# Two steps of a recurrent stage's key normalisation move by one level each, on TensorE and on VectorE

## What is computed

```python
def wkv_scan(state0, r, dec, k, v, kk, a, reverse):
    def step(S, inp):
        d_t, k_t, v_t, kk_t, a_t = inp[:5]
        sa = jnp.einsum("bhvk,bhk->bhv", S, -kk_t)
        S = (S * d_t[:, :, None, :] + sa[..., None] * (kk_t * a_t)[:, :, None, :]
             + v_t[..., None] * k_t[:, :, None, :])
        out = jnp.einsum("bhvk,bhk->bhv", S, inp[5])
        return S, out
```

```python
    kk = heads(k * k_k).astype(jnp.float32)
    kk = kk * lax.rsqrt(jnp.sum(kk * kk, axis=-1, keepdims=True) + 1e-12)
```

## Time and profile before

| | us |
|---|---|
| median of 3 runs (4238.46 to 4240.1) | 4239.78 |
| the profiled execution | 4227.17 |
| its span, first to last instruction | 4225.4 |
| the recurrent stage's 120 levels in it, at 2353 to 3057 | 704 |

### The profile page before, as it was taken

One profiled execution on the slowest core, in us unless ns is written; L12 is line 12 of the kernel. 1 busy time (PEld: TensorE's weight loads), 2 busy tenths in 40 slices (PEclk: granted clock), 3 DMA queues, 4 the chain that ended last, 5 costly groups with the idle time before them and its releaser, 6 DMA issues. The chain is left out here.

```text
span 4225.4 us, 73949 instructions
## 1 busy us (share of the span) xinstructions
PE 3967.2 (94%) x32724; PEld 2597.9 (61%) x32724; DVE 1985.2 (47%) x3187; ACT 953.8 (23%) x1726; POOL 739.3 (17%) x598
## 2 busy tenths in 40 slices
PE   7999999999999999999998788888899999999997
PEld 2458886454788855555555677777754555554443
DVE  2547813365585149734101355555423544541593
ACT  2411100010120020021003443434213434430102
POOL 0024542000444410001001222332010100002000
PEclk9999999999999999999998999999999999999999
DMA  1123323432442212012223311111101111111121
GB/s 62 41 95 139 111 89 139 150 120 99 141 149 80 70 53 67 30 40 92 101 77 130 108 45 38 34 34 34 77 34 52 47 51 54 48 58 49 60 70 40
DMA packets 119124, 317.98 MB, mean 75 GB/s; under 512 B 12128, under 2 KB 79712, under 8 KB 107296
## 3 DMA queue, kind: packets, MB, share of 16 engines
q1 hardware_dynamic: 113040, 291.37, 19.8%
q0 software_dynamic: 5776, 22.03, 1.6%
HBM read 276.67 MB, written 30.41 MB: 73 GB/s over the span
## 5 line engine op out<-in xcount | busy, mean ns | idle before, releaser
L782 PE MATMUL lin_ps<-hn,ring 128*128 128x512 f32 (+1 forms) x4384 | 1457.1, 489 | 24.3 <-ACT arena L1650 8.8
L782 PEld LDWEIGHTS lin_ps<-hn,ring 128*128 128x128 f32 x4384 | 829.2, 190 | 604.0 <-issue 542.9
L782 PE MATMUL lin_ps<-arena,ring 128*128 128x256 f32 (+2 forms) x3056 | 950.4, 468 | 9.6 <-DVE arena L2589 7.6
L782 PEld LDWEIGHTS lin_ps<-arena,ring 128*128 128x128 f32 (+1 forms) x3056 | 577.8, 190 | 358.8 <-issue 305.4
L782 PE MATMUL lin_ps<-arena 64*64 64x64 f32 (+3 forms) x9432 | 623.0, 254 | 68.6 <-ACT arena L1650 30.6
L1650 ACT ACTIVATE arena<-lin_ps 128x512 f32<-128x512 f32 (+4 forms) x533 | 280.4, 546 | 1272.2 <-PE lin_ps L782 1271.9
L782 PEld LDWEIGHTS lin_ps<-arena 64*64 64x64 f32 (+1 forms) x9432 | 466.6, 142 | 158.9 <-issue 88.3
L2198 DVE SCALAR_TENSOR_TENSOR arena<-arena,vec 128x512 f32<-128x512 f32 (+3 forms) x499 | 386.5, 858 | 149.3 <-PE lin_ps L782 148.0
L782 PE MATMUL sum_ps<-arena 64*64 64x64 f32 (+1 forms) x7176 | 313.1, 223 | 34.9 <-issue 23.0
L2198 DVE SCALAR_TENSOR_TENSOR arena<-arena,cs 128x512 f32<-128x512 f32 x336 | 327.1, 1044 | 0.0
L782 PEld LDWEIGHTS sum_ps<-arena 64*64 64x64 f32 (+1 forms) x7176 | 263.2, 136 | 45.8 <-issue 27.7
(11 more groups left out here) (219 smaller groups left out, 3711.4 us busy)
## 6 DMA issues: line engine op xcount, KB each, us to landing
ring<-w_up SPq DMA_DIRECT2D x32, 1024.0 KB, 5.8
ring<-w_down SPq DMA_DIRECT2D x32, 1024.0 KB, 5.0
arena<-w_mod SPq DMA_DIRECT2D x24, 1024.0 KB, 7.8
arena<-w_mod SPq DMA_DIRECT2D x12, 2048.0 KB, 7.6
ring<-w_attn SPq DMA_DIRECT2D x16, 1536.0 KB, 6.7
ring<-w_conv_in SPq DMA_DIRECT2D x16, 1024.0 KB, 5.8
ring<-features SPq DMA_DIRECT2D x40, 384.0 KB, 3.4
features<-arena POOLq DMA_DIRECT2D x32, 384.0 KB, 2.6
```

Source lines behind the costliest of these rows:

```text
L782: return pe.matmul(out, lhsT, rhs, start=start, stop=stop)
```

## The change

Two tuples in the two `aside` functions:

```diff
@@ TensorE, aside(G, l)
                 if j + 1 < KD:
                     if (gg, l) == (0, 1):
                         key_sums(j + 1)
-                    if (gg, l) in ((0, 3), (0, 5)):
+                    if (gg, l) in ((0, 4), (0, 5)):
                         key_spread(j + 1, l // 5)
@@ VectorE, aside(G, l)
                     if (gg, l) == (0, 4):
                         keys(j + 1, 0)
-                    if (gg, l) == (1, 2):
+                    if (gg, l) == (1, 1):
                         keys(j + 1, 1)
```

## The result

| | before | change |
|---|---|---|
| median of five executions each, us | 4239.43 | 4197.07 |
| lowest to highest | 4233.45 to 4240.10 | 4192.83 to 4203.18 |
| the profiled execution | 4227.17 | 4203.18 |
| 120 levels of the stage, first to last level_z, in the profiled execution | 703.9 | 678.6 |
| TensorE's "issue" waits in the stage | 51.8 | 63.9 |

The ratio is 0.9908, with a 95% interval of 0.9897 to 0.9918. The change is faster by 42.4 us between medians, by some 39 us by the ratio. I had forecast 30.0 us and a range that ended at 4201: right in direction, too small in size. Two later comparisons gave 0.9917 (0.9904 to 0.9931) and 0.9904 (0.9886 to 0.9922), 32.5 and 39.4 us between medians. Two executions of the kernel before in those comparisons, of 5312.98 and 14702.32 us, ran in a slow state and are in none of the medians and means given here.

A forecast was written before the change was run, and what follows sets the result against it. TensorE, busy 94% of the span, was taken as the bound, its idle waits as lost time. Terms 12.2 + 13.5 + 7.6 + 3.7 = 37.0 us freed, less 7.0: 4239.8 - 30.0 = 4209.8 us, range 4201 to 4221.

The forecast's parts named there:

- The two waits: TensorE's waits on the reciprocal at (0,3) and the keys at (1,2) would go, freeing 12.2 and 13.5 us.
- The row that was to show the order: New TensorE waits on the keys would disprove 0.9 us of room; waits on L2696 or L2701 would show VectorE late.
- The spread's own time: The spread's 1.09 us would fall into 1.29 us of idle time ahead of level 5, freeing 7.6 us.
- GpSimd: Its wait on the keys would go from 24.6 us to near 0, worth 0 because TensorE never waits on it.
- The hold: New TensorE waits for instruction blocks behind the moved spread, one of mean length per cycle, would give back 7.0 us.
- The clock: Falls to 1.2 GHz behind the wait at (0,3), in three of seven cycles, would go, freeing 3.7 us.
- From profile to median: The profiled execution lay 12.6 us under the median; the same 30.0 us was taken off the median, giving 4209.8 us.

The follow-up runs named there:

- the shifted blocks: The change with 128 more TensorE instructions, half a block, in idle time ahead of its untouched recurrent stage; measured 0.9916 (0.9894 to 0.9939) of the kernel before.
- The repeated kernel before: The kernel before, run again with no edit; measured median 4233.73 us, ratio 0.9997 (0.9988 to 1.0006).
- the two repeats: The kernel before and the change, each run again with no edit; measured medians 4233.73 us and 4201.67 us.
- The spread alone: The kernel before with only the spread of part 0 moved from (0,3) to (0,4), keys left at (1,2); measured 0.9957 (0.9945 to 0.9969).
- the keys alone: The kernel before with only the second half of the keys moved from (1,2) to (1,1), spread left at (0,3); measured 0.9955 (0.9943 to 0.9967).

## Why the prediction was right or wrong

- **The two waits** (12.2 and 13.5 us): right, both gone, in every profile with the move. The row that was to show the order, no new wait on the keys or on late merges: right.
- **The spread's own time** (7.6 us): right. By the table of waits it looks smaller: the masks' waits went (2.2 us), ScalarE's shrank by 0.50 us in seven cycles (3.5 us), together 5.7 us. But the time from the start of one product to the start of another says more. From the last product of E at (0,4) to that at (0,5) it is 6.7 to 6.9 us before. In the change, with the spread between them, it is 6.7 us in five of the seven cycles; in the other two new holds of 0.67 and 1.01 us stand in it. So the spread costs nothing at its new place, and at (0,3) the stretch without its waits is shorter by 1.1 to 1.2 us (in cycles 1 and 2, at 2.4 GHz throughout, 2.8 instead of 3.95 us). Where products overlap, waits shrink by less than the time of the work that fills them.
- **GpSimd** no longer waits for the keys, and none of TensorE's waits named it before or after, as said. For what it may mean to VectorE see the last section.
- **The hold** (7.0 us): the mechanism was right and is now shown by the shifted blocks and the packets. Behind the spread, from the end of (0,3) to the end of (0,4), the "issue" waits grew by 6.2 us, near the 7.0. But the sum had no holds behind the moved keys, and from (1,2) to (1,4) they grew by 5.3 us; in all it is 12.1 us in the profile. The prediction took two neighbouring ends of blocks to be 3.7 us apart at the least; with waits at both, they come as close as 3.4 us. It is also here that the rule of the Trainium skill cited in the prediction (Runtime: NRT & Kernel Launch, section Instruction fetch mechanics) fails for this kernel: crossing a block is hidden at 96 of 165 ends in the change's stage, and the other 69 cost 63.9 us.
- **The clock** (3.7 us, bounds 0 and 3.7): this step failed. I counted falls in one execution, behind (0,3) only, and called their number the upper bound. The repeated kernel before has 44.4 us at 1.2 GHz in its stage, not 20.5, and five of its falls stand behind the keys' wait at (1,2), which the sum gave no clock at all. The changed kernel has 13.7 to 17.1 us. At 0.35 us for each, the clock gave 1.2 us between the first two profiles and 10.7 us between the two repeats.
- **From profile to median**: here the failed step turned into the miss. "since nothing here depends on the run, I take the same off the median": the profiled execution lay 12.6 us under the median of its kernel, and that difference was in large part made of what the change removes. The hint stood in the table, and I read it as a constant.

Net: without the clock the sum would be 12.2 + 13.5 + 7.6 - 7.0 = 26.3 us. The stages of the profiles give 21 to 24 us: the holds cost 5.1 us more than the sum had, and waits on ScalarE at (1,2) and (1,4) shrank by 2.4 us without being in it. The table by clock gives 26 to 29 us for the whole execution; which of the two is nearer is not shown. On top come some 8 us of clock in the later sessions, more than twice the term. So the errors partly cancel, and luck has its part in the number too: the repeats of the change have medians of 4201.67 and 4197.20 us, on both sides of the range's end. For the first session's before no clock was recorded for each timed execution; that its 42.4 us contain still more of it is likely and not shown.

## What to carry to other kernels

Where a wait stands in front of dense work, its price is its length plus what the clock loses behind it in a share of executions, so take the number of falls from several executions, and ask of a profile that lies under the median what it lacks. With many short matmuls count instructions too: the time between block ends gives a second floor, and each wait removed brings the kernel closer to it, behind every step that moves and not only the first. To price work that moves into idle time, compare the starts of the rows around it, not the table of waits. Steps of an aside belong where their engine waits anyway, behind the instruction that starts that wait.

## What the runs showed of the hardware

- TensorE's instructions come in blocks of 256. All 52, 69 and 67 "issue" waits of the three kernels counted stand at the end of a block, and each ends 0.9 to 1.6 us after a packet of instructions has landed. Where two neighbouring ends both have a wait, they are at least 3.4 us apart, mostly 3.4 to 4.2 us. Where TensorE had not run up against the supply, a block went by in less: at 2701.30 of the change a whole one, 133 matmuls by the view of windows, took 2.44 us without a wait.
- Useless products in a wait made the whole kernel faster, 0.9988 (0.9979 to 0.9997), and at equal clock left the stage at the same 696.8 us.
- A product of 64x64 with two columns is not nearly free: 64 matmuls with their weight loads took 2.0 us, 32 ns each, where 26 matmuls of 64 columns in `values` took 0.97 us, 37 ns each, and those of the 2.44 us above, nearly all of 64 columns too, 18 ns each.
- The time of VectorE's 128x768 addition at L2758 goes with what GpSimd does beside it. It took 0.95 us in the two cycles in which GpSimd does nothing meanwhile, 1.5 to 1.6 us with GpSimd busy for 1.0 to 1.1 us of it (before), and 1.7 to 1.8 us with 1.3 to 1.6 us (the change). The spread alone gives the longer time, the keys alone the shorter. That GpSimd is the cause is not shown by a run of its own. The 0.23 us more in the cycle shown more than cover what the keys at (1,1) left less of room than predicted, 0.31 instead of 0.46 us.
